# Moving two of seven low-part subtractions per set from VectorE to GpSimd in a fp32 Strassen-Winograd MLP product

## The chip, the cores and the metric

One Trainium2 chip (trn2), one core. The metric is the device time of one execution in microseconds (us), lower is better.

## The reference, cut to what matters

The program is one step of a two-layer backbone on 512 latent and 128 context tokens (640 in all, width 1024). Each layer ends in an MLP with a gated residual:

```python
h2 = _rms_norm(x, lp['norm2_g']) * (1 + sc2) + sh2
x = x + g2 * (jnp.square(jax.nn.relu(h2 @ lp['w_ff1'])) @ lp['w_ff2'])
```

`w_ff1` is 1024 x 4096 and `w_ff2` is 4096 x 1024, all in float32. The change lies in the product with `w_ff2` of the second layer.

## The kernel before, in words

The kernel feeds TensorE with fp32r operands. To keep the precision of a float32 product, it splits each operand in a high part, the value cast to fp32r, and a low part, the value minus its high part. A product is then three matmuls: high by high, high by low, low by high.

**The second MLP.** The second layer's MLP does both of its products in the Strassen-Winograd way: seven block products and a number of block sums take the place of eight block products. The work is 32 *pairs* p (p = 0 to 15 for `w_ff1`, p = 16 to 31 for `w_ff2`), and each pair is seven *products* i = 0 to 6 of 12 matmuls (4 slices of the contraction by 3 parts), so one product is 12 matmuls. A running number w = 7p + i counts the products. The hidden activations of the first product are squared, combined into seven block operands and stored to memory in `hb`. The second product goes through them in four *sets* (c = 0 to 3) of seven *stored blocks* (i = 0 to 6, 128 x 1280 each). Set c is used by the four pairs from p = 16 + 4c on, and its block i is the moving operand of product i of each of them.

**How a set is made ready.** In the pair before the set (p = 15 + 4c) and in the set's first pair, block i is loaded by SP's queue to a stage `FS`, ScalarE casts it to the high part `FB[i][:, 0]` (`block_split`, semaphore `fbh`), and VectorE subtracts to make the low part `FB[i][:, 1]` (`stored_lo`, semaphore `fbv`). TensorE waits for `fbv` before product i of the set's first pair. In what follows, *step r* of a set is the product number counted from the start of pair 15 + 4c: r = 0 to 6 is that pair, and r = 7 + i is the product that first uses block i. The orders are written out by hand: `SPLIT_AT` says at which step ScalarE casts a block, `AT_STEP` at which step VectorE subtracts it (for sets 1 to 3 blocks 0 to 6 at steps 2, 4, 6, 7, 8, 9, 11), and `LATE` by how much the splitting of the weights is held back in these steps.

**What else the engines do.** For each product, VectorE makes the low part of a weight slice (`weight_lo`, `WHL<-RAWB,WHL`, 128 x 512, semaphore `wlo`), for which TensorE waits before each product. These are called WHL r here after the step whose product needs them. In each pair VectorE also forms sums with PSUM: `sums` at i = 3 (`U<-PS,E` and `U<-PS,U`), `lower_right` at i = 5 (`TMP<-PS,U` of L1627, which product 6 of the same pair waits for by `c22`), `upper_right` at i = 6 (`c12`, for product 1 of the next pair) and `lower_left` (`c21`). VectorE runs all of this in one order, as do the others.

**GpSimd.** In pairs p > 16 GpSimd adds three blocks of the pair before into the residual (`residuals(p - 1)`, 128 x 320, L760): the first after ScalarE's first `gated`, the other two after the second. In pairs up to 16 it forms `hidden_sums(p - 1)`, four operations of 128 x 320. For each pair the loop goes on only when these are done. `lower_right(p)` waits by `xup` for the residuals of the pair before.

A stage is used again by a later block. In set 0, where only stages 0 to 3 serve the first seven blocks, the load of block 6 waits for the low part of block 2, in SP's queue between the loads of weights.

Of the kernel before, what the change touches and what calls it, by code (L numbers as in the profile page):

```python
# [7 lines left out]
F32 = mybir.dt.float32  # L8
F32R = mybir.dt.float32r
ALU = mybir.AluOpType  # L10
# [14 lines left out]
H = 4  # L25
# [54 lines left out]
PAIRS7 = 32  # L80
HALF = PAIRS7 // 2
PRODUCTS = 7
SLOTS = 8
BW = 336
SHIFTED = (0, 3, 4, 6)
BX = HT + 2
# [21 lines left out]
def rotations():  # L108
# [27 lines left out]
    ada_mm=8, ada_ev=8, ada_tr=8, mod_done=1, moda_done=2)  # L136

FPER = dict(
    hr=8, hbt=16, hbh=28, hbl=28, sxr=1, sxh=3, sxl=3, whi=7 * PAIRS7, wlo=7 * PAIRS7, pp=7 * PAIRS7,
    e1=PAIRS7, u2=PAIRS7, u4=PAIRS7, c11=PAIRS7, c12=PAIRS7, c21=PAIRS7, c22=PAIRS7, z1=HALF, z2=2 * HALF,  # L140
    fre=PAIRS7, fsq=PAIRS7, ft=4 * HALF, fo0=48 * HALF // 2, fo1=48 * HALF // 2, fs0=80, fs1=80, fs2=80, fs3=64, fs4=48, fs5=48, fs6=48, fbh=28, fbv=28,
    xup=3 * HALF, gt=2 * (HALF - 1), lsq=3)

LENT = dict(
    hr="tap", hbt="taps", hbh="conv", hbl="silu", sxr="csq", sxh="css", sxl="crt", fs3="crr", fs4="o_sq", fs5="o_rt", fs6="ors", whi="kdm", wlo="kde", pp="gce",
# [4 lines left out]
def build(nc, t):  # L150

    ctx = ExitStack()
    with ctx:
# [239 lines left out]
        F = {n: S[x] for n, x in LENT.items()}  # L393
# [27 lines left out]
        def stage(n):  # L421

            return n % 4 if n < PRODUCTS else n % PRODUCTS

        def stage_turn(n):

            return len([x for x in range(n) if stage(x) == stage(n)])
# [66 lines left out]
        with nc.Block() as block:  # L494

            @block.sync
            def _(sp):
# [19 lines left out]
                def fast_loads(l):  # L517

                    b, g0 = fast_base(l), l * CHUNKS + 16

                    def hidden_out(p):

                        c, e = divmod(p, H)
                        done = F["fo1" if p % 2 else "fo0"]
                        sp.wait_ge(F["fsq"], b["fsq"] + 2 * p + 2)
                        sp.dma_start(t["hb"][c, 0, :, e, :], SQ[p % 2][:, 0, 0, :]).then_inc(done, 16)
                        sp.dma_start(t["hb"][c, 1:3, :, e, :].rearrange("b p t -> p b t"), SQ[p % 2][:, 1, :, :]).then_inc(done, 16)
                        sp.wait_ge(F["ft"], b["ft"] + 4 * p + 4)
                        sp.dma_start(t["hb"][c, 3:7, :, e, :].rearrange("b p t -> p b t"), TT4[:, :, :]).then_inc(done, 16)

                    def block_in(n):

                        c, i = divmod(n, PRODUCTS)
                        if i == 0:
                            for x in ("fo0", "fo1"):
                                sp.wait_ge(F[x], b[x] + 48 * (2 * c + 2))
                        if c and i == 4:
                            for x in ("fo0", "fo1"):
                                sp.wait_ge(F[x], b[x] + 24 * HALF)
                        if stage_turn(n):  # L540
                            sp.wait_ge(F["fbv"], b["fbv"] + max(x for x in range(n) if stage(x) == stage(n)) + 1)
                        sp.dma_start(FS[stage(n)][:, :, :], t["hb"][c, STORED[i]]).then_inc(F[f"fs{stage(n)}"], 16)

                    def weights_in(w):

                        p, i = divmod(w, PRODUCTS)
                        if i in PLAIN:
                            src = t["ws"][g0 + p, 32 * PLAIN[i]:32 * PLAIN[i] + 32, :]
                        else:
                            src = t["wp"][SUMMED[i], p]  # L550
                        sp.dma_start(RAWB[:, w % SLOTS, :], src.rearrange("r (a c) -> (r a) c", a=4)).then_inc(slot_in[w % SLOTS], 16)
                    for w in range(SLOTS):
                        if w % 4 == 0:
                            sp.wait_ge(lo_ready, g0 - 1 + w // 4)
                        if w == 1:
                            sp.wait_ge(sums_added, 16 * PAIRS7)
                        weights_in(w)
                    for w in range(7 * PAIRS7):
                        if w + SLOTS < 7 * PAIRS7:
                            sp.wait_ge(F["wlo"], b["wlo"] + w + 1)  # L560
                            weights_in(w + SLOTS)
                        p, i = divmod(w, PRODUCTS)
                        if i == (3 if p == HALF else 5) and 2 <= p < HALF + 2:
                            hidden_out(p - 2)
                        c, k = divmod(w - 7 * (HALF - 3), 28)
                        if 0 <= c < 4:
                            at_step = (6, 8, 10, 12, 22, 23, 23) if c == 0 else (4, 6, 8, 10, 12, 14, 16)
                            for i in range(PRODUCTS):
                                if at_step[i] == k:
                                    block_in(7 * c + i)  # L570
# [149 lines left out]
            def _(pool):  # L720

                def square_sum(n, x, tmp=None, ks=range(KT)):

                    c = squared(n)
                    tmp = TC[0][:, 0:T] if tmp is None else tmp
                    for k in ks:
                        t_ = x(k)
                        if k == 0:
                            nc.gpsimd.tensor_tensor(SQA[:, :], t_, t_, ALU.mult).then_inc(nsq, 1)
                            continue  # L730
                        nc.gpsimd.tensor_tensor(tmp, t_, t_, ALU.mult).then_inc(nsq, 1)
                        pool.wait_ge(nsq, c + 2 * k)
                        nc.gpsimd.tensor_tensor(SQA[:, :], SQA[:, :], tmp, ALU.add).then_inc(nsq, 1)
                        pool.wait_ge(nsq, c + 2 * k + 1)

                def fast_mlp(l, x):
# [25 lines left out]
                    def finished(j, p):  # L762
# [2 lines left out]
                        pool.wait_ge(F["xup"], b["xup"] + 3 * (p - HALF + 1))  # L765
                        square_sum(2 * l + 2, lambda k: flat(X[:, (k % 2) * H + k // 2, :, :]), ks=range(2 * j, 2 * j + 2))
                    square_sum(2 * l + 1, x, SQX[:, :], range(KT - 1))
                    for p in range(PAIRS7):
                        if p > HALF:
                            residuals(p - 1)  # L770
                        if 1 <= p <= HALF:
                            hidden_sums(p - 1)
                        if p > PAIRS7 - 4:
                            finished(p - 1 - (PAIRS7 - 4), p - 1)
# [701 lines left out]
            def _(dve):  # L1476
# [41 lines left out]
                def fast_mlp(l, residual):  # L1518
# [155 lines left out]
                    for w in range(7 * PAIRS7):  # L1674
# [33 lines left out]
                            shift_rest(2, 6, 1).then_inc(F["sxl"], 1)  # L1708
                        c = (p - HALF + 1) // 4
                        rel = w - 7 * (HALF - 1 + 4 * c) if 0 <= c < 4 else -1  # L1710
                        if rel in AT_STEP[c > 0]:
                            stored_lo(7 * c + AT_STEP[c > 0][rel])
                        while low[0] < min(7 * PAIRS7, w + 1 + LO_AHEAD - LATE[c > 0].get(rel, 0)):
                            weight_lo(low[0])
# [554 lines left out]
            def _(pe):  # L2269
# [44 lines left out]
                def fast_mlp(l):  # L2314
# [3 lines left out]
                    def product(w):  # L2318
# [24 lines left out]
                            pe.wait_ge(F["c22"], b["c22"] + p + 1)  # L2343
                        if second and p % 4 == 0:
                            c = (p - HALF) // 4
                            pe.wait_ge(F["fbv"], b["fbv"] + 7 * c + i + 1)
                        out = bank(BANKS[i])[:, 0:n]
                        hi, lo = WHL[:, w % SLOTS, 0, :], WHL[:, w % SLOTS, 1, :]
                        B = HB[i] if first else FB[i]
# [622 lines left out]
```

## Time and profile before

| | us |
|---|---|
| median of 3 runs | 1829.47 (1827.41 to 1832.43) |
| the profiled execution, its own time | 1830.21 |
| its span (first to last instruction) | 1828.4 |
| TensorE busy | 1745.6 (95% of the span) |
| VectorE busy | 1274.1 (70%) |
| ScalarE busy | 841.6 (46%) |
| GpSimd busy | 526.1 (29%) |
| low parts of the stored blocks on VectorE, 28 of them | 1.478 median each |

The span is what the trace covers, and the profiled execution's own time has 1.8 us around it. Busy shares are averages over stages with different limits. The second product of the second MLP runs from 1607.4 to 1813.4 us of the span.

### The profile page before, as it was taken

How to read it: one execution, taken by the hardware profiler on the slowest of the kernel's cores; microseconds unless marked ns; L12 is line 12 of the kernel's file. 1: busy time of each engine (PE TensorE's matmuls, PEld its weight loads, DVE VectorE, ACT ScalarE, POOL GpSimd, SP SyncE). 2: the span in 40 equal slices, each digit the busy share in tenths (PEclk: the TensorE clock that was granted, in tenths of full speed). 3: DMA queues.
4: the chain of work that ended last, by engine and by line, in shares of the span. 5: the costliest groups of instructions: out<-in, count | busy, mean ns of one | idle time of the engine just before them, and what ended most of it. 6: DMA issues, size and time to landing. Idle time of an engine off the chain costs nothing.

```text
span 1828.4 us, 33566 instructions
## 1 busy us (share of the span) xinstructions
PE 1745.6 (95%) x13554; PEld 1659.0 (91%) x13554; DVE 1274.1 (70%) x2127; ACT 841.6 (46%) x1459; POOL 526.1 (29%) x424
## 2 busy tenths in 40 slices
PE   5999999998999999999999999898989999999997
PEld 2989986787999999999999999677889999989997
DVE  2688785688635677676764557666977777788886
ACT  1555327634242231322325653475436666666664
POOL 5000011085442050331551000204832232232225
PEclk9999999989999999999999999998999999999998
DMA  8653223022367869687627761541122677886662
GB/s 345 245 209 95 77 81 59 1 65 88 149 235 209 295 230 321 244 272 273 194 90 203 182 151 47 139 93 42 48 95 90 218 233 256 292 281 245 218 225 88
DMA packets 128038, 316.66 MB, mean 173 GB/s; under 512 B 37829, under 2 KB 64237, under 8 KB 108173
## 3 DMA queue, kind: packets, MB, share of 16 engines
q1 hardware_dynamic: 121740, 279.49, 43.5%
q0 software_dynamic: 4608, 33.56, 9.5%
q8 instruction: 108, 1.77, 0.4%
q10 hardware_dynamic: 1536, 1.48, 0.2%
q14 instruction: 46, 0.37, 0.1%
HBM read 286.01 MB, written 95.49 MB: 209 GB/s over the span
## 4 chain that ended last, share of the span: by engine, by line
PE 78%; DVE 9%; DMA 4%; issue 3%; POOL 3%; ACT 2%; SPq 1%; POOLq 0%; ACTq 0%; DVEq 0%
PE PS L2288 47%; PE PS L2357 17%; DMA ADA<-ada 2%; PE PS L2562 1%; PE PS L2650 1%; POOL FL L911 1%; PE PS L2611 1%; DVE WHL L1544 1%; PE PS L2590 1%; PE PS L2579 1%; PE PS L2724 1%; DVE MPR L1750 1%; PE PS L2425 1%; PE PS L2599 1%; DMA RAWB<-ws 1%
## 5 line engine op out<-in xcount | busy, mean ns | idle before, releaser
L2288 PE MATMUL PS<-HH,HI 128*128 128x320 f32 (+1 forms) x1280 | 300.4, 316 | 4.6 <-DVE HL L1499 4.6
L2288 PE MATMUL PS<-HL,HI 128*128 128x320 f32 (+1 forms) x1280 | 295.9, 313 | 0.0
L2288 PE MATMUL PS<-HH,LO 128*128 128x320 f32 (+1 forms) x1280 | 294.3, 311 | 0.0
L952 ACT CAST HI<-RAW 128x2048 fp32r<-128x2048 f32 x64 | 121.9, 1904 | 273.9 <-PE PS L2288 246.9
L2288 PEld LDWEIGHTS PS<-HH,HI 128*128 128x128 f32 x1280 | 215.8, 191 | 5.2 <-issue 5.1
L2288 PEld LDWEIGHTS PS<-HL,HI 128*128 128x128 f32 x1280 | 219.7, 192 | 0.0
L2288 PEld LDWEIGHTS PS<-HH,LO 128*128 128x128 f32 x1280 | 217.5, 191 | 0.0
L2357 PE MATMUL PS<-FB,WHL 128*128 128x320 f32 x1344 | 199.6, 310 | 6.7 <-DVE TMP L1627 4.3
L2357 PEld LDWEIGHTS PS<-FB,WHL 128*128 128x128 f32 x1344 | 197.1, 188 | 9.1 <-DVE WHL L1544 7.7
L2357 PE MATMUL PS<-HB,WHL 128*128 128x322 f32 (+1 forms) x1344 | 201.5, 313 | 2.4 <-DVE TMP L1627 1.4
L2357 PEld LDWEIGHTS PS<-HB,WHL 128*128 128x128 f32 x1344 | 200.5, 190 | 3.1 <-issue 3.1
L1490 DVE TENSOR_TENSOR LO<-RAW,HI 128x2048 fp32r<-128x2048 f32 (+1 forms) x66 | 155.2, 2352 | 57.5 <-ACT HI L952 57.2
L999 ACT CAST WHL<-RAWB 128x512 fp32r<-128x512 f32 x224 | 137.8, 619 | 112.4 <-PE PS L2357 94.5
L2288 PE MATMUL PS<-FH,HI 128*128 128x320 f32 x768 | 176.6, 311 | 1.6 <-issue 1.6
L1544 DVE TENSOR_TENSOR WHL<-RAWB,WHL 128x512 fp32r<-128x512 f32 x224 | 169.3, 781 | 11.7 <-ACT WHL L999 10.0
L2288 PE MATMUL PS<-FH,LO 128*128 128x320 f32 x768 | 175.1, 309 | 0.0
L2288 PE MATMUL PS<-FL,HI 128*128 128x320 f32 x640 | 146.4, 310 | 0.0
L1750 DVE SCALAR_TENSOR_TENSOR MPR<-WM,CB 128x1024 f32<-128x1024 f32 x96 | 137.9, 1436 | 11.2 <-DMA WM<-adt 9.5
L2288 PEld LDWEIGHTS PS<-FH,HI 128*128 128x128 f32 x768 | 128.5, 189 | 2.0 <-issue 1.1
L2288 PEld LDWEIGHTS PS<-FH,LO 128*128 128x128 f32 x768 | 128.7, 188 | 0.0
L2288 PEld LDWEIGHTS PS<-FL,HI 128*128 128x128 f32 x640 | 107.5, 189 | 0.0
L928 POOL TENSOR_TENSOR TC<-TC 128x640 f32<-128x640 f32 x32 | 50.4, 1576 | 181.1 <-ACT FH L1435 181.1
(347 smaller groups left out, 2902.7 us busy)
## 6 DMA issues: line engine op xcount, KB each, us to landing
RAW<-ws SPq DMA_DIRECT2D x64, 1024.0 KB, 5.1
wp<-ws SPq DMA_DIRECT2D x32, 1024.0 KB, 8.2
RAWB<-wp SPq DMA_DIRECT2D x128, 256.0 KB, 3.9
WM<-adt SPq DMA_DIRECT2D x48, 512.0 KB, 9.4
RAWB<-ws SPq DMA_DIRECT2D x96, 256.0 KB, 3.6
FS<-hb SPq DMA_DIRECT2D x28, 640.0 KB, 8.0
ADA<-ada SPq DMA_DIRECT2D x16, 1024.0 KB, 7.7
wp<-ws POOLq DMA_DIRECT2D x16, 1024.0 KB, 10.1
```

What stands on the lines that cost most here:

```text
L911: last = nc.gpsimd.tensor_tensor(grp(halves(FL, j), g), nat(ATT[:, j, :], g, g * LAT), grp(halves(FH, j), g).bitcast(F32), ALU.subtract)
L928: nc.gpsimd.tensor_tensor(TC[u][:, 0:T], TC[u][:, 0:T], TC[u][:, 0:T], ALU.mult).then_inc(S["f1_sq"], 1)
L952: nc.scalar.copy(HI[g % 2][:, :], RAW[g % 2][:, :]).then_inc(hi_ready, 1)
L999: nc.scalar.copy(WHL[:, w % SLOTS, 0, :], operand(w)).then_inc(F["whi"], 1)
L1490: last = nc.vector.tensor_tensor(LO[g % 2][:, c], RAW[g % 2][:, c], HI[g % 2][:, c].bitcast(F32), ALU.subtract)
L1544: nc.vector.tensor_tensor(WHL[:, w % SLOTS, 1, :], operand(w), WHL[:, w % SLOTS, 0, :].bitcast(F32), ALU.subtract).then_inc(F["wlo"], 1)
L1750: return nc.vector.scalar_tensor_tensor(out=MPR[:, :], in0=w[:, :], scalar=1.0, in1=cond[:, g, :], op0=ALU.mult, op1=ALU.mult, accum_out=M ...
L2288: last = pe.matmul(bank(2 * u + a)[:, 0:e], w[:, cols], m[:, a * HT:a * HT + e], start=(k == 0 and f), stop=(k == KT - 1 and e_))
L2357: last = pe.matmul(out, x[:, cols], B[:, y, k, 0:n], start=(opens and k == 0 and v == 0), stop=(k == H - 1 and v == 2), skip_group_check=n ...
L2425: last = pe.matmul(bank(7)[:, 464 + i * NB + b:465 + i * NB + b], SQT[i % 2][:, c.start - 1:c.stop - 1], one, start=True, stop=True)
L2562: pe.matmul(pair(0)[:, 0:LAT], q, kt[:, 0:LAT], start=True, stop=True)
L2579: last = pe.matmul(bank(7 if i else 2)[:, c:c + hi - lo], TSQ[rows, p, toks(b)], KSW[rows, lo:hi], start=True, stop=True)
```

## The change

Of the seven stored blocks of a set, blocks 2 and 5 (`POOLED`) get their low part on GpSimd: eight subtractions of 128 x 1280 in all. VectorE's order leaves these two steps out and is otherwise the same. In GpSimd's loop, at the set's first pair (p = 16, 20, 24, 28), block 2 stands ahead of that iteration's residual additions, and block 5 behind them and ahead of the hidden sums (of p = 16 alone, where there are no additions yet). The new subtractions count on the semaphore `hbt`. TensorE and SP wait for whichever semaphore the block now has (`low_done`).

```diff
+POOLED = (2, 5)
...
+        def low_done(b, n):
+
+            c, i = divmod(n, PRODUCTS)
+            if i in POOLED:
+                return F["hbt"], b["hbt"] + 16 + len(POOLED) * c + POOLED.index(i) + 1
+            return F["fbv"], b["fbv"] + (PRODUCTS - len(POOLED)) * c + i + 1 - len([x for x in POOLED if x < i])
...
-                            sp.wait_ge(F["fbv"], b["fbv"] + max(x for x in range(n) if stage(x) == stage(n)) + 1)
+                            sp.wait_ge(*low_done(b, max(x for x in range(n) if stage(x) == stage(n))))
...
+                    def stored_lo(n):
+
+                        i = n % PRODUCTS
+                        pool.wait_ge(F["fbh"], b["fbh"] + n + 1)
+                        nc.gpsimd.tensor_tensor(FB[i][:, 1, :, :], FS[stage(n)][:, :, :], FB[i][:, 0, :, :].bitcast(F32),
+                                                ALU.subtract).then_inc(F["hbt"], 1)
                     for p in range(PAIRS7):
+                        c, first = divmod(p - HALF, H)
+                        if c >= 0 and first == 0:
+                            stored_lo(PRODUCTS * c + POOLED[0])
                         if p > HALF:
                             residuals(p - 1)
+                        if c >= 0 and first == 0:
+                            stored_lo(PRODUCTS * c + POOLED[1])
                         if 1 <= p <= HALF:
                             hidden_sums(p - 1)
...
-                        if rel in AT_STEP[c > 0]:
+                        if rel in AT_STEP[c > 0] and AT_STEP[c > 0][rel] not in POOLED:
                             stored_lo(7 * c + AT_STEP[c > 0][rel])
...
-                            pe.wait_ge(F["fbv"], b["fbv"] + 7 * c + i + 1)
+                            pe.wait_ge(*low_done(b, 7 * c + i))
```

## Rows read from the trace of the kernel before

**Rows 1.** The chain of work that ended last: share of the span by engine

```profile
PE 78%; DVE 9%; DMA 4%; issue 3%; POOL 3%; ACT 2%; SPq 1%; POOLq 0%; ACTq 0%; DVEq 0%
```

**Rows 2.** Busy time by stretch: length, then PE, PEld, DVE, ACT, POOL, clock, DMA

```profile
1675.00:1697.00 22.00, 22.00 (x152) 22.00 (x151) 16.24 (x29) 11.22 (x22) 5.69 (x6) 1.00 0.97 359
1697.00:1725.00 28.00, 26.99 (x183) 26.52 (x182) 24.26 (x35) 20.60 (x32) 7.93 (x6) 1.00 0.43 141
```

**Rows 3.** Timeline of TensorE, second product: start, us, what [idle before]

```profile
1607.43 8.96 PE L2357 MATMUL PS<-FB,WHL 128*128 128x320 f32 x60
1617.05 2.03 PE L2357 MATMUL PS<-FB,WHL 128*128 128x320 f32 x12 [0.66 <-DVE WHL L1544]
1620.22 24.86 PE L2357 MATMUL PS<-FB,WHL 128*128 128x320 f32 x168 [1.15 <-DVE FB L1667]
...
1710.21 12.55 PE L2357 MATMUL PS<-FB,WHL 128*128 128x320 f32 x84 [0.80 <-DVE TMP L1627]
1722.98 37.18 PE L2357 MATMUL PS<-FB,WHL 128*128 128x320 f32 x252 [0.22 <-issue]
```

**Rows 4.** The low parts of the stored blocks, all 28: min/median/max ns

```profile
L1667 DVE TENSOR_TENSOR FB<-FS,FB x28: 1471/1478/2164, 1597.5 to 1770.4; 128x1280 fp32r<-128x1280 f32 x28
```

**Rows 5.** Timeline of VectorE around set 2

```profile
1707.59 1.48 DVE L1667 TENSOR_TENSOR FB<-FS,FB 128x1280 fp32r<-128x1280 f32 x1
1708.99 0.68 DVE L1544 TENSOR_TENSOR WHL<-RAWB,WHL 128x512 fp32r<-128x512 f32 x1
1709.59 0.47 DVE L1627 TENSOR_TENSOR TMP<-PS,U 128x320 f32<-128x320 f32 x1
...
1710.58 0.67 DVE L1544 TENSOR_TENSOR WHL<-RAWB,WHL 128x512 fp32r<-128x512 f32 x1
...
1713.38 4.28 DVE L1667 TENSOR_TENSOR FB<-FS,FB 128x1280 fp32r<-128x1280 f32 x3
...
1718.61 1.18 DVE L1544 TENSOR_TENSOR WHL<-RAWB,WHL 128x512 fp32r<-128x512 f32 x1
1719.71 2.16 DVE L1667 TENSOR_TENSOR FB<-FS,FB 128x1280 fp32r<-128x1280 f32 x1
...
1722.40 0.47 DVE L1627 TENSOR_TENSOR TMP<-PS,U 128x320 f32<-128x320 f32 x1
```

**Rows 6.** Timeline of ScalarE around set 2

```profile
1706.94 1.27 ACT L1071 CAST FB<-FS 128x1280 fp32r<-128x1280 f32 x1
...
1716.35 1.01 ACT L1079 ACTIVATE TMP<-TMP,MOD 128x512 f32<-128x512 f32 x2
```

**Rows 7.** Timeline of GpSimd around set 2: first and third residual addition

```profile
1715.67 2.73 POOL L760 TENSOR_TENSOR X<-X,TMP 128x320 f32<-128x320 f32 x1 [8.56 <-ACT TMP L1079]
...
1719.20 1.32 POOL L760 TENSOR_TENSOR X<-X,TMP 128x320 f32<-128x320 f32 x1
```

**Rows 8.** GpSimd's subtractions in the first MLP, its residual additions: min/median/max ns

```profile
L931 POOL TENSOR_TENSOR FL<-TC,FH x32: 1559/1578/2432, 525.3 to 908.8; 128x640 fp32r<-128x640 f32 x32
...
L760 POOL TENSOR_TENSOR X<-X,TMP x45: 870/882/2728, 1625.7 to 1806.1; 128x320 f32<-128x320 f32 x45
```

**Rows 9.** Timelines of VectorE and GpSimd behind set 0

```profile
1625.41 1.97 DVE L1544 TENSOR_TENSOR WHL<-RAWB,WHL 128x512 fp32r<-128x512 f32 x2
...
1625.68 1.15 POOL L760 TENSOR_TENSOR X<-X,TMP 128x320 f32<-128x320 f32 x1 [1.35 <-ACT TMP L1079]
```

**Rows 10.** Timelines of GpSimd, ScalarE and VectorE at set 0

```profile
1605.82 1.40 POOL L752 TENSOR_TENSOR TT<-SQ,TT 128x320 f32<-128x320 f32 x1
...
1613.42 1.25 ACT L1071 CAST FB<-FS 128x1280 fp32r<-128x1280 f32 x1
...
1614.90 1.49 DVE L1667 TENSOR_TENSOR FB<-FS,FB 128x1280 fp32r<-128x1280 f32 x1
1616.31 1.28 DVE L1544 TENSOR_TENSOR WHL<-RAWB,WHL 128x512 fp32r<-128x512 f32 x2
```

**Rows 11.** DMA issues from 1608 to 1611 us: count, KB each, us to landing

```profile
FS<-hb SPq DMA_DIRECT2D x1, 640.0 KB, 5.2
```

More of the change, by code:

```diff
@@ L138 @@
 FPER = dict(
-    hr=8, hbt=16, hbh=28, hbl=28, sxr=1, sxh=3, sxl=3, whi=7 * PAIRS7, wlo=7 * PAIRS7, pp=7 * PAIRS7,
+    hr=8, hbt=16 + 4 * len(POOLED), hbh=28, hbl=28, sxr=1, sxh=3, sxl=3, whi=7 * PAIRS7, wlo=7 * PAIRS7, pp=7 * PAIRS7,
     e1=PAIRS7, u2=PAIRS7, u4=PAIRS7, c11=PAIRS7, c12=PAIRS7, c21=PAIRS7, c22=PAIRS7, z1=HALF, z2=2 * HALF,
-    fre=PAIRS7, fsq=PAIRS7, ft=4 * HALF, fo0=48 * HALF // 2, fo1=48 * HALF // 2, fs0=80, fs1=80, fs2=80, fs3=64, fs4=48, fs5=48, fs6=48, fbh=28, fbv=28,
+    fre=PAIRS7, fsq=PAIRS7, ft=4 * HALF, fo0=48 * HALF // 2, fo1=48 * HALF // 2, fs0=80, fs1=80, fs2=80, fs3=64, fs4=48, fs5=48, fs6=48, fbh=28, fbv=28 - 4 * len(POOLED),
     xup=3 * HALF, gt=2 * (HALF - 1), lsq=3)
```

## The prediction

> **What bounds the kernel now.** I read the chain that ended last first: TensorE holds 78% of it [rows 1]. A cut on another engine pays only where TensorE waits for it. The stretches show where that is [rows 2]: between two sets TensorE is busy for 22.00 of 22.00 us, and in the stretch around set 2 for 26.99 of 28.00 us, with the clock at 1.00 in both. So the timeline of TensorE comes next [rows 3]. From step 6 of set 2 it runs 84 matmuls in 12.55 us, or 1.79 us for a product of 12, and around the sets it waits. In set 0 it waits 0.66 us at step 12 (the 60 matmuls of steps 7 to 11 end at 1616.4) and 1.15 us at step 13. In set 2 it waits 0.80 us ahead of step 6 and 0.22 us ahead of step 13, and sets 1 and 3 repeat set 2 with other offsets. The 0.80 us end with VectorE's L1627 of step 5, which stands behind block 1 and a weight [rows 5]; both stay on VectorE. What the change could give back is thus 0.66 + 1.15 + 3 x 0.22 = 2.5 us at most. This is under 0.3% of the time (5.5 us), about what a measurement of this kernel can tell from no change.
>
> **What is removed.** Eight subtractions of 1.48 us [rows 4] leave VectorE: 11.8 us of its time. By itself this is worth at most the 2.5 us above, for elsewhere TensorE is behind its own work.
>
> **What is added, and its length.** GpSimd gets eight subtractions of 128 x 1280, which it hasn't done before. Its nearest row is the same operation with the same types on 128 x 640: 1.56 us undisturbed. A two-input operation on 128 x 320 takes 0.87 us [rows 8]. So 320 elements cost 0.69 us, and 1280 make 1.56 + 2 x 0.69 = 2.94 us. The bounds are 1.56 (no longer than half the elements) and 3.12 us (twice the half); 1.56 would mean that the growth from 320 to 640 stops there, so I take 2.94.
>
> **The two engines shut each other out.** In set 2 GpSimd's first addition began at 1715.67 and took 2.73 us where 0.88 is usual [rows 7, 8]; VectorE's three subtractions in a row meanwhile ran unstretched until 1717.66 [rows 5]. Then it was VectorE's turn to lose: the weight at 1718.61 took 1.18 us for 0.67, and block 6 at 1719.71 took 2.16 for 1.48 [rows 4, 5], while GpSimd's additions ran. The excess of each is the other's remainder, to about 0.1 us. VectorE's operations with PSUM show no such stretch (0.47 us). I take from this that an operation of GpSimd and one of VectorE with both inputs in SBUF don't run side by side, and that the one that comes second waits for the whole of the first.
>
> The Trainium skill says so too (SBUF — State Buffer, SBUF: two separate sides): the port pair that VectorE and GpSimd share is an exclusive lock, and a VectorE instruction with two SBUF inputs is among those that want it. By that rule moving work from VectorE to GpSimd frees VectorE of 1.48 us and blocks it for GpSimd's whole operation; the trace agrees, with the 2.73 us above. Without the lock the sum would be the 3 us of the second rival, with it the 7.3 us below.
>
> **Block 2 in sets 1 to 3.** In set 2 its cast ends at 1706.94 + 1.27 = 1708.21 [rows 6], and GpSimd has done the additions of the pair before. But VectorE subtracts block 1 until 1709.07, and the weight WHL 10 follows at once until 1709.67 [rows 5]. Which of the two gets the turn at 1709.0 is open. In favour of VectorE: at 1716.2 GpSimd had waited for 0.5 us, and VectorE's next block still went first (2.73 us) [rows 7]. In favour of GpSimd: at 1626.1 it had waited for 0.4 us and got in between two weights, which took 1.97 us instead of 1.3 [rows 9]. Block 1 is of the first kind, long and with the next instruction ready, so I let VectorE go first. Then GpSimd runs from about 1709.6 to 1712.5. L1627 reads PSUM and isn't held up. Behind it the next weight at 1710.58 waits until 1712.4 and ends at 1713.05; upper_right ends at 1713.5, in time for step 8 at 1713.8. Block 2 is due at 1715.6. Cost: nothing, hidden behind steps 6 to 8 with 0.2 us to spare. If GpSimd goes first, WHL 10 and L1627 end 2.7 us later, and TensorE's step 6 with them: 2.7 us a set.
>
> **Block 5 in sets 1 to 3.** It stands behind three additions. The first begins when block 4 on VectorE ends (now about 1716.6, as blocks 3 and 4 run 0.4 us later than before without block 2) and ends at 1717.4. The other two want ScalarE's second product with the gate, done at 1716.35 + 1.01 = 1717.36 [rows 6], and take until 1717.4 + 2 x 0.87 = 1719.1. The weight WHL 12, ready at 1718.61, waits for that and runs to 1719.6. Then block 5 takes until 1719.5 + 2.94 = 1722.45. Step 12 was at 1710.21 + 6 x 1.79 = 1720.95; with 0.15 us of signal, as from L1627's end at 1710.06 to 1710.21, it starts at 1722.6, or 1.65 us late. Behind block 5 VectorE has block 6 (until 1723.8), WHL 13 (1724.4) and L1627 (1724.8), in one queue; TensorE's step 13 waits for the last, so it starts at 1724.95 instead of 1722.98: 2.0 us late a set, the stall at step 12 included. If block 6 goes ahead of block 5, both come later by 1.5 to 2 us, 3.9 us a set; if the lock costs nothing, 1.0 us (second rival). Later steps follow with the same shift, as TensorE ran 252 matmuls without a wait behind it [rows 3], so nothing gives this back.
>
> **Set 0.** There are no additions, so block 2 starts when GpSimd's hidden sums end at 1607.2 and ends at 1610.2, before step 9 at 1611.0; VectorE's block 3 waits behind it, but is due only at 1612.8. SP's load of block 6 now waits for this end instead of VectorE's at 1608.7; it takes 5.2 us [rows 11] and lands at 1615.4, before its cast at 1617.3, so I cost it at nothing (it would cost TensorE directly if it landed 2 us later). Block 5's cast ends at 1613.42 + 1.25 = 1614.67 [rows 10]; GpSimd subtracts until 1617.6. VectorE, without block 5 at 1614.90, wants the weight of step 12 at once, but is shut out until 1617.6 and ends it at 1618.2. Step 12 starts at 1618.35 instead of 1617.05: 1.3 us, and step 13 follows between 0.85 and 1.7 us late. I take 1.3.
>
> **The sum.** 3 x 2.0 + 1.3 = 7.3 us. The profiled execution took 1830.21 us (its span 1828.4), so it would take 1837.5; it stands 0.74 us above the median of the runs. From the median I predict 1829.5 + 7.3 = 1836.8 us.
>
> **Rivals.**
>
> *GpSimd goes first with block 2.* Its 2.7 us ahead of step 6 come on top of block 5's wait, which stays at 2.0 us: 4.7 x 3 + 1.3 = 15.4 us, 1844.9 us. For it speaks the case at 1626 us, against it the one at 1716 us. All three sets should go the same way, as their offsets are alike.
>
> *The lock costs nothing at the critical places.* Then block 5 still can't start before the additions end at 1719.1, and ends at 1722.0; step 12 comes 1.2 us and step 13 1.0 us late, and in set 0 step 12's 0.7 us vanish in the old wait at step 13. The sum is 3 x 1.0 = 3.0 us, 1832.5 us, within 0.3%. Against it stand the stretched rows; for it, that VectorE's operations with PSUM fill part of these steps and aren't stretched.
>
> *GpSimd is in time, not slower.* If its subtraction takes under 1.8 us (from 1719.1 to 1720.9), block 5 is there at step 12, the earlier VectorE wins the 2.5 us, and the time is 1827.0 us. The 1.56 us for half the elements speaks against it.
>
> *The change does nothing for TensorE either way* would need both waits hidden; the additions ahead of block 5 exclude it unless the operation is as short as in the last rival.
>
> **Chances and range.** The forecast 0.47, GpSimd first 0.30, no lock 0.18, in time 0.05. The forecast itself lies between 4.5 us (0.8 less for each set) and 13 us (block 6 goes first: 3 x 3.9 + 1.3), so a sixth of it, 0.08, falls within 0.3%. Faster by over 0.3% would need 5.5 us where 2.5 are to be had: 0.02. Within 0.3%: 0.18 + 0.05 + 0.08 - 0.02 = 0.29. Slower: the rest, 0.69. The range of 8 in 10 runs from just below the no-lock case, 1832.0, to above GpSimd first with 0.7 us more a set, 1847.0; of the likeliest alone it is 1834 to 1842.
>
> **What would show it.** In the changed profile: GpSimd's 128 x 1280 subtractions of about 2.9 us, longer where VectorE had the turn; VectorE's weights stretched to 2 us and more behind them; TensorE waiting 1.6 us at step 12 of sets 1 to 3 and L1627 behind block 6 ahead of step 13; no longer wait ahead of step 6 (a wait of 3.5 us there is the first rival); in set 0 a wait of about 2 us at step 12 for a weight. The prediction is wrong if GpSimd's operation is much shorter or longer than 2.94 us (0.1 us of it is 0.4 us of the sum), if the additions end earlier than 1719.1, or if VectorE's queue falls behind by so much that weights come late in later pairs, which the DMA's long stretches could turn into further waits.

## The result and the profile after

The changed kernel takes 1853.89 us (median of 4 runs, 1852.97 to 1855.22) beside 1830.11 us of the kernel before in the same session (4 runs): a ratio of 1.0129 [1.0114, 1.0144], slower by 23.8 us. The forecast was 1836.8 us in a range of 1832.0 to 1847.0: the direction was right, and the time lies 6.9 us outside the range. The profiled execution took 1853.50 us with a span of 1851.7 us, so its span is 23.3 us longer than before.

The lines of the kernel have moved: L1686 is VectorE's low part of a block (L1667 before), L780 GpSimd's, L1563 the low part of a weight, L1646 `lower_right`, L768 the residual additions and L2376 TensorE. In the other runs they shift again, by a few lines.

Timeline of TensorE in the changed kernel, second product, from step 12 of set 0 to behind set 2 (answers to [rows 3]):

```profile
1618.03 2.02 PE L2376 MATMUL PS<-FB,WHL 128*128 128x320 f32 x12 [1.89 <-DVE WHL L1563]
1621.26 37.32 PE L2376 MATMUL PS<-FB,WHL 128*128 128x320 f32 x252 [1.20 <-DVE FB L1686]
1662.08 13.47 PE L2376 MATMUL PS<-FB,WHL 128*128 128x320 f32 x72 [3.50 <-DVE TMP L1646]
1677.17 2.00 PE L2376 MATMUL PS<-FB,WHL 128*128 128x320 f32 x12 [1.62 <-POOL FB L780]
1679.48 37.18 PE L2376 MATMUL PS<-FB,WHL 128*128 128x320 f32 x252 [0.31 <-issue]
1720.16 13.45 PE L2376 MATMUL PS<-FB,WHL 128*128 128x320 f32 x72 [3.50 <-DVE TMP L1646]
1735.23 2.00 PE L2376 MATMUL PS<-FB,WHL 128*128 128x320 f32 x12 [1.62 <-POOL FB L780]
1737.54 37.18 PE L2376 MATMUL PS<-FB,WHL 128*128 128x320 f32 x252 [0.31 <-issue]
1778.22 13.43 PE L2376 MATMUL PS<-FB,WHL 128*128 128x320 f32 x72 [3.51 <-DVE TMP L1646]
```

Three things are to be seen. Ahead of step 6 of each later set TensorE now waits 3.50 us. Behind that wait the 72 matmuls of steps 6 to 11 take 13.45 us, though the same number took 72/84 of 12.55 = 10.76 us before [rows 3]. And step 12 waits 1.62 us, this time for GpSimd. For set 1, whose rows of before don't stand above, the timeline of TensorE in the kernel before had this:

```profile
1645.68 12.55 PE L2357 MATMUL PS<-FB,WHL 128*128 128x320 f32 x84 [0.59 <-DVE TMP L1627]
1659.48 12.55 PE L2357 MATMUL PS<-FB,WHL 128*128 128x320 f32 x84 [1.25 <-DVE TMP L1627]
```

Timeline of VectorE in the changed kernel around set 2: block 1, the weight of step 10, `lower_right` of step 5; further on the weight of step 12 and block 6 (answers to [rows 5]):

```profile
1714.83 1.48 DVE L1686 TENSOR_TENSOR FB<-FS,FB 128x1280 fp32r<-128x1280 f32 x1
1716.23 3.38 DVE L1563 TENSOR_TENSOR WHL<-RAWB,WHL 128x512 fp32r<-128x512 f32 x1
1719.54 0.48 DVE L1646 TENSOR_TENSOR TMP<-PS,U 128x320 f32<-128x320 f32 x1
...
1731.18 1.12 DVE L1563 TENSOR_TENSOR WHL<-RAWB,WHL 128x512 fp32r<-128x512 f32 x1
1732.23 4.21 DVE L1686 TENSOR_TENSOR FB<-FS,FB 128x1280 fp32r<-128x1280 f32 x1
```

Timeline of GpSimd in the same stretch: block 2, the last two additions, block 5 (answers to [rows 7]):

```profile
1715.52 3.55 POOL L780 TENSOR_TENSOR FB<-FS,FB 128x1280 fp32r<-128x1280 f32 x1 [1.16 <-ACT FB L1090]
...
1730.04 1.71 POOL L768 TENSOR_TENSOR X<-X,TMP 128x320 f32<-128x320 f32 x2 [0.88 <-ACT TMP L1098]
1731.72 3.36 POOL L780 TENSOR_TENSOR FB<-FS,FB 128x1280 fp32r<-128x1280 f32 x1
```

Block 2 is there at 1715.52, while VectorE still subtracts block 1. When block 1 ends at 1716.31, GpSimd goes first, and the weight of step 10, which stands next on VectorE (1716.23), needs 3.38 us instead of 0.68. `lower_right` stands behind it, and TensorE's step 6 waits for `lower_right`.

Busy time by stretch in the changed kernel, behind the wait of set 2: length, then PE, PEld, DVE, ACT, POOL, granted clock, DMA (answers to [rows 2]):

```profile
1720.00:1722.00 2.00, 1.84 (x7) 1.87 (x8) 1.60 (x5) 0.00 (x0) 0.00 (x0) 0.50 0.37 131
1722.00:1725.00 3.00, 3.00 (x13) 3.00 (x12) 1.26 (x2) 1.21 (x2) 0.00 (x0) 0.50 0.40 93
1725.00:1728.00 3.00, 3.00 (x19) 3.00 (x18) 2.04 (x2) 1.96 (x5) 0.00 (x0) 0.82 0.01 3
1728.00:1731.00 3.00, 3.00 (x23) 3.00 (x22) 0.83 (x2) 2.56 (x6) 1.84 (x3) 1.00 0.00 0
```

After the wait TensorE has the granted clock 0.50, the lower of its two levels (1.2 GHz), and 1.00 (2.4 GHz) again later; 0.82 is a mean of the two. At 0.50 it does 13 matmuls in 3 us, at 1.00 it does 23.

**Where the 23.3 us are.** From step 6 of set 0 to the end of the last product it took 1813.58 - 1605.56 = 208.0 us before and takes 1835.56 - 1605.32 = 230.2 us now: 22.2 us more. They are, set by set from the rows above:

| place | us |
|---|---|
| wait ahead of step 6: 3.50 + 3.50 + 3.51 instead of 1.25 + 0.80 + 0.79 | +7.7 |
| steps 6 to 11 at half clock: 13.47 + 13.45 + 13.43 instead of 3 x 10.76 | +8.1 |
| step 12: 3 x 1.62 of wait, and 2.00 for the 12 matmuls that start anew instead of 1.79 | +5.5 |
| step 13: 3 x 0.31 instead of 0.21 + 0.22 + 0.21 | +0.3 |
| set 0: 1.89 and 1.20 instead of 0.66 and 1.15 | +1.3 |
| the wait of 0.59 us between sets 0 and 1 that is gone, and 0.1 more in the last pair | -0.5 |

This makes 22.4, within 0.2 us of the 22.2. The rest of the span, 1.3 us behind the last product less 0.2 us ahead of set 0, lies where the change does nothing. Behind the last product TensorE is busy for 6.70 us instead of 5.40, at a mean clock of 0.60 instead of 0.68: its last two groups of ten small matmuls take 2.04 and 2.39 us instead of 1.26 and 1.86, which is these 1.3 us. The 2.39 us also stand in `writes_without_reads` below, which is as fast as the kernel before, so that part, 0.5 us, can't be put down to the change.

### The profile page after: what moved, and what is told of

Same layout as the page of the kernel before. It is cut to its first block, busy times and chain, and to the rows that moved or that the text cites. A ratio compares the mean times of both kernels' runs of the same rounds, so it can differ in the third digit from the quotient of the medians.

```text
span 1851.7 us, 33566 instructions
## 1 busy us (share of the span) xinstructions
PE 1751.8 (95%) x13554; PEld 1665.9 (90%) x13554; DVE 1282.3 (69%) x2119; ACT 842.0 (45%) x1459; POOL 545.9 (29%) x432
## 3 DMA queue, kind: packets, MB, share of 16 engines
q10 hardware_dynamic: 1536, 1.48, 0.2%
## 4 chain that ended last, share of the span: by engine, by line
PE 77%; DVE 9%; issue 4%; POOL 3%; DMA 3%; ACT 2%; SPq 1%; POOLq 0%; DVEq 0%; ACTq 0%
PE PS L2307 46%; PE PS L2376 18%; DMA ADA<-ada 2%; PE PS L2581 1%; DVE WHL L1563 1%; POOL FL L930 1%; PE PS L2630 1%; PE PS L2609 1%; PE PS L2669 1%; PE PS L2598 1%; PE PS L2743 1%; DVE MPR L1769 1%; PE PS L2444 1%; PE PS L2618 1%; PE PS L2642 1%
## 5 line engine op out<-in xcount | busy, mean ns | idle before, releaser
L2376 PE MATMUL PS<-FB,WHL 128*128 128x320 f32 x1344 | 208.2, 317 | 20.4 <-DVE TMP L1646 11.5
L2376 PEld LDWEIGHTS PS<-FB,WHL 128*128 128x128 f32 x1344 | 205.1, 195 | 23.3 <-DVE WHL L1563 16.2
L2376 PE MATMUL PS<-HB,WHL 128*128 128x322 f32 (+1 forms) x1344 | 201.3, 312 | 2.6 <-DVE TMP L1646 1.4
L2376 PEld LDWEIGHTS PS<-HB,WHL 128*128 128x128 f32 x1344 | 200.3, 190 | 3.3 <-issue 3.3
L1563 DVE TENSOR_TENSOR WHL<-RAWB,WHL 128x512 fp32r<-128x512 f32 x224 | 179.4, 826 | 9.6 <-ACT WHL L1018 8.1
L1769 DVE SCALAR_TENSOR_TENSOR MPR<-WM,CB 128x1024 f32<-128x1024 f32 x96 | 137.9, 1437 | 11.8 <-DMA WM<-adt 10.1
```

What stands on the lines that cost most here:

```text
L1563: nc.vector.tensor_tensor(WHL[:, w % SLOTS, 1, :], operand(w), WHL[:, w % SLOTS, 0, :].bitcast(F32), ALU.subtract).then_inc(F["wlo"], 1)
L1769: return nc.vector.scalar_tensor_tensor(out=MPR[:, :], in0=w[:, :], scalar=1.0, in1=cond[:, g, :], op0=ALU.mult, op1=ALU.mult, accum_out=M ...
L2376: last = pe.matmul(out, x[:, cols], B[:, y, k, 0:n], start=(opens and k == 0 and v == 0), stop=(k == H - 1 and v == 2), skip_group_check=n ...
```

## The experiments

Ratios are against the kernel before, run beside each. "Held" below means the time that one engine shuts the other out.

### The two blocks apart

`block5_alone` leaves block 2 on VectorE, `block2_alone` block 5; the rest is as in the changed kernel.

```diff
-POOLED = (2, 5)
+POOLED = (5,)      # block5_alone: behind the additions; block2_alone has (2,), ahead of them
...
```

> Only block 5 goes to GpSimd, block 2 stays on VectorE. Theory (GpSimd takes its turn between block 1 and the next weight on VectorE, TensorE pauses for 3.5 us ahead of step 6, and its clock falls for that pause): no extra pause ahead of step 6 (0.8 us as before), the clock stays at 1.00 between the sets, block 5 costs 1.6 to 2.0 us in each of sets 1 to 3 and 1.2 us in set 0, in all 6 to 8 us: 1836 to 1838 us. Rival (the clock falls for the pause of 1.6 us at step 12, or for anything else that came with the change): the half clock shows in this run too and the time is 1843 us or more.

> Only block 2 goes to GpSimd. Theory: the pause of 3.5 us ahead of step 6 in sets 1 to 3 stays, with the fall of the clock behind it (2.7 + 2.7 us a set, 16 us), no wait at step 12 for GpSimd, set 0 as before or 0.5 us better: 1845 to 1847 us. Rival (block 2 and block 5 hurt only together, or the fall of the clock belongs to block 5): 1838 us or less.

With block 5 alone the time is 1837.56 us, ratio 1.0037 [1.0023, 1.0052]; with block 2 alone 1843.02 us, ratio 1.0067 [1.0043, 1.0091]. TensorE's timelines, first block 5 alone, then block 2 alone:

```profile
1713.42 10.80 PE L2374 MATMUL PS<-FB,WHL 128*128 128x320 f32 x72 [0.79 <-DVE TMP L1644]
1725.84 2.00 PE L2374 MATMUL PS<-FB,WHL 128*128 128x320 f32 x12 [1.62 <-POOL FB L780]
1728.15 37.18 PE L2374 MATMUL PS<-FB,WHL 128*128 128x320 f32 x252 [0.31 <-issue]
```

```profile
1663.61 52.14 PE L2374 MATMUL PS<-FB,WHL 128*128 128x320 f32 x336 [3.50 <-DVE TMP L1644]
1719.25 51.03 PE L2374 MATMUL PS<-FB,WHL 128*128 128x320 f32 x336 [3.50 <-DVE TMP L1644]
1773.78 26.41 PE L2374 MATMUL PS<-FB,WHL 128*128 128x320 f32 x168 [3.50 <-DVE TMP L1644]
```

The waits belong to the blocks one by one: 3.50 us to block 2, 1.62 us to block 5. The half clock goes with the 3.50 us (72 matmuls take 10.80 us behind a wait of 0.79). Here it took less than in the changed kernel: 336 matmuls at full clock are 4 x 12.55 = 50.2 us, so 1.9, 0.8 and 1.3 us went; why the clock came back sooner here, no run tells. The execution in this trace took 1846.05 us, within the 1845 to 1847 us expected, but it was the slowest of four: the median is 2 us under what I expected, and there is no trace of a faster one.

### Is it the wait that halves the clock?

`filled_pause` is the changed kernel with 20 matmuls of no use in TensorE ahead of step 6, so that the wait is as long, but TensorE works in it.

```diff
 if i == 6:
+    if p in (19, 23, 27):
+        for _ in range(20):
+            pe.matmul(bank(7)[:, 0:HT], WHL[:, w % SLOTS, 0, 0:P], WHL[:, w % SLOTS, 0, 0:HT], start=True, stop=True)
     pe.wait_ge(F["c22"], b["c22"] + p + 1)
```

> The changed kernel, and TensorE runs 20 matmuls of no use (operands that are there, a bank of PSUM that nobody reads) in its pause ahead of step 6 of sets 1 to 3. Nothing else is altered, step 6 can start no earlier. Theory (the idle pause lets the clock fall, which costs 2.7 us a set behind it): granted clock 1.00 in steps 6 to 11, their 72 matmuls take 10.8 us instead of 13.5, and the time falls by 8 us to 1845.8 us. Rival (the fall has another cause): 1853 to 1854 us and the half clock as before.

It takes 1846.37 us, ratio 1.0086 [1.0065, 1.0108], so 7.5 us less than the changed kernel with 60 matmuls more. TensorE's timeline, and the busy time of the stretch behind it:

```profile
1656.79 3.10 PE L2364 MATMUL PS<-WHL 128*128 128x320 f32 x20
1660.44 10.82 PE L2380 MATMUL PS<-FB,WHL 128*128 128x320 f32 x72 [0.55 <-DVE TMP L1646]
```

```profile
1660.40:1671.30 10.90, 10.82 (x72) 10.55 (x72) 8.31 (x11) 7.22 (x12) 4.50 (x4) 1.00 0.20 51
```

The wait for VectorE is about the same (1660.44 - 1656.79 = 3.65 us), but the clock stays at 1.00 and the 72 matmuls take 10.82 us, in all three sets (10.82, 10.82 and 10.83). So the 8.1 us are the price of an idle TensorE, and they come on top of the wait itself.

### Does GpSimd hold VectorE for one instruction?

`halves` cuts each of GpSimd's subtractions into two of 128 x 640.

```diff
...
-nc.gpsimd.tensor_tensor(FB[i][:, 1, :, :], FS[stage(n)][:, :, :], FB[i][:, 0, :, :].bitcast(F32), ALU.subtract).then_inc(F["hbt"], 1)
+for h in (slice(0, 2), slice(2, 4)):
+    nc.gpsimd.tensor_tensor(FB[i][:, 1, h, :], FS[stage(n)][:, h, :], FB[i][:, 0, h, :].bitcast(F32), ALU.subtract).then_inc(F["hbt"], 1)
```

> The changed kernel with each of GpSimd's subtractions cut in two of 128 x 640 (1.56 us each by the rows of the first MLP). Theory (the turn at the SBUF port is held for one instruction): VectorE gets the weight of step 10 in behind the first half, so the pause ahead of step 6 is about 0.8 + 1.35 = 2.2 us instead of 3.5; block 6 on VectorE gets in between the halves of block 5, so the wait at step 12 grows to about 3 us and the one at step 13 goes. Whether the clock falls for pauses of 2.2 and 3 us is open; without it 1843 to 1846 us, with it up to 1853. Rival (the turn is held until GpSimd has nothing waiting): pauses as before, 1853 us.

It takes 1851.96 us, ratio 1.0119 [1.0106, 1.0133]. TensorE's timeline in set 1:

```profile
1662.54 10.79 PE L2377 MATMUL PS<-FB,WHL 128*128 128x320 f32 x72 [2.16 <-DVE TMP L1647]
1676.34 41.56 PE L2377 MATMUL PS<-FB,WHL 128*128 128x320 f32 x264 [3.01 <-POOL FB L781]
```

The wait ahead of step 6 shrinks to 2.16 us, as the weight of step 10 now waits for one half (2.03 us instead of 3.38) and gets its turn between the two. But block 5 pays: VectorE gets in between its halves too, and step 12 waits 3.01 us. The lock is held for one instruction, and what is cut up loses its place. The total hardly falls, since TensorE's clock now drops behind the three waits of 3.01 us and behind one of the three of 2.15 us: the 264 matmuls above take 41.56 us where 22 products of 1.79 us would be 39.4.

`port_held_without_use` and `writes_without_reads` are the kernel before with an operation of no use on GpSimd in sets 1 and 2, at the place of block 2, for which no other engine waits. The first reads constants and subtracts, the second only writes.

```diff
 ...
+if p in (20, 24):
+    pool.wait_ge(F["fbh"], b["fbh"] + 7 * (p - HALF) // 4 + 3)
+    nc.gpsimd.tensor_tensor(DUM[:, :], K[:, 0:1152], K[:, 0:1152], ALU.subtract) ...   # port_held_without_use
+    for k in range(3): nc.gpsimd.memset(DUM[:, :], 0.0) ...                            # writes_without_reads
     ...
```

> The kernel before, with all low parts on VectorE, and in sets 1 and 2 GpSimd subtracts 128 x 1152 constants into a place that nobody reads, at the point where the change has block 2 (2.65 us long by the same slope). No other engine waits for it. Theory (it is the turn at the port that hurts, not data that come late): TensorE pauses 0.8 + 2.4 = 3.2 us ahead of step 6 in sets 1 and 2, set 3 as before; with half clock behind the pauses between 0.8 and 2.7 us each, 1836 to 1840 us. Rival (block 2 on GpSimd hurts since its result comes late): 1830 us, as before.

> The same, but GpSimd runs three memsets of 128 x 1152 into the unused place instead, about 1 us each, one after the other: it writes SBUF and reads none. Theory in the form of the Trainium skill (VectorE with two SBUF inputs is shut out only by a GpSimd operation that reads SBUF): the pause ahead of step 6 stays 0.8 us and the time 1830 us. Rival (any work of GpSimd in SBUF shuts VectorE out): WHL 10 is stretched by up to 1 us and step 6 late by as much in sets 1 and 2, 1832 us or more, and the stretch shows in the rows.

The first takes 1836.05 us, ratio 1.0033 [1.0023, 1.0043]; the second 1831.28 us, ratio 1.0001 [0.9992, 1.001]. Timelines of all engines in set 2 give GpSimd's operation and VectorE's block 1 and weight, first with the subtraction, then with the writes:

```profile
1710.32 1.48 DVE L1672 TENSOR_TENSOR FB<-FS,FB 128x1280 fp32r<-128x1280 f32 x1
...
1711.02 2.74 POOL L772 TENSOR_TENSOR DUM<-K 128x1152 f32<-128x1152 f32 x1 [1.18 <-ACT FB L1076]
...
1711.72 2.59 DVE L1549 TENSOR_TENSOR WHL<-RAWB,WHL 128x512 fp32r<-128x512 f32 x1
```

```profile
1706.84 1.48 DVE L1673 TENSOR_TENSOR FB<-FS,FB 128x1280 fp32r<-128x1280 f32 x1
...
1707.52 3.30 POOL L773 MEMSET DUM<- 128x1152 f32 x3 [1.16 <-ACT FB L1077]
...
1708.24 0.68 DVE L1550 TENSOR_TENSOR WHL<-RAWB,WHL 128x512 fp32r<-128x512 f32 x1
```

The subtraction that nobody needs makes the weight 2.59 us and step 6 wait 2.71 us in both sets (0.80 in set 3, where it isn't done); three writes of 3.30 us together make no difference. The 2.71 us are less than the 3.2 expected because this subtraction of constants ran only 1.96 us past block 1's end (1711.02 + 2.74 - 1711.80), where block 2 ran 2.76 us past it in the changed kernel. So it is no dependence on block 2 that delays step 6, but the reading GpSimd. The Trainium skill (SBUF — State Buffer, SBUF: two separate sides) says that a VectorE operation with two SBUF inputs contends only with a GpSimd operation that reads SBUF; these two runs agree with it.

### Who gets the turn

`block2_a_little_later` and `block2_much_later` are the changed kernel with a clearing of 128 x 256 and of 128 x 704 unused elements in front of block 2's subtraction in sets 1 to 3. `three_arrivals` and `arrivals_late` are the kernel before with a subtraction of no use at block 2's place behind nothing or a clearing; each set has a size of its own.

```diff
 if c >= 0 and first == 0:
+    if c:
+        pool.wait_ge(F["fbh"], b["fbh"] + PRODUCTS * c + POOLED[0] + 1)
+        nc.gpsimd.memset(DUM[:, 0:256], 0.0)        # much later: 0:704
     stored_lo(PRODUCTS * c + POOLED[0])
```

> As the changed kernel, but in sets 1 to 3 GpSimd clears 128 x 256 unused elements (an operation without an SBUF input, about 0.3 us) between block 2's cast and its subtraction, and nothing else waits for that. My reading of the rows: who gets the turn is settled before VectorE's running instruction ends; GpSimd got in when it came at most 0.70 us after that instruction had begun, and not when it came 0.79 us after or later. Block 2 came 0.69 us after block 1 had begun; 0.3 us later it should lose the turn to the weight of step 10: the pause ahead of step 6 is 0.8 us in place of 3.5, the clock doesn't fall, and the kernel with a longer GpSimd path is some 16 us faster: about 1837.5 us. Rival: GpSimd gets the turn at any end of a VectorE instruction for which it waits at all; then the pause is 3.5 us again, the clock falls, and the time is about 1854 us.

> The kernel before, with a subtraction of 128 x 896 constants on GpSimd at block 2's place in sets 1, 2 and 3 that nobody waits for: in set 1 at once after block 2's cast, in set 2 behind a clearing of 128 x 32 elements (estimate 0.1 to 0.2 us), in set 3 behind one of 128 x 256 (0.3 us). If the turn is settled some 0.7 us after block 1 begins, set 1 has a weight of step 10 of about 2 us and a pause of 2.1 us ahead of step 6, set 3 has 0.68 and 0.80 us, and set 2 is on the edge. Rival (any wait is enough): all three sets have the long weight and the pause.

> As the run with block 2 a little later, but with 128 x 704 elements cleared (estimate 0.7 us): GpSimd then comes about 1.3 us after block 1 has begun, some 0.1 to 0.2 us before its end. If there is a point near the end from which VectorE's next instruction goes first, the weight of step 10 takes 0.68 us, the pause ahead of step 6 is 0.8 us, and the time about 1838 us. If any wait is enough for GpSimd: weight about 3.1 us, pause 3.5 us (what GpSimd loses by the clearing is hidden in block 1), about 1853 us.

> The kernel before, with a short subtraction of 128 x 288 constants (about 0.8 us) that nobody waits for, behind clearings of 128 x 384, 576 and 768 elements in sets 1, 2 and 3: it comes about 1.1, 1.25 and 1.4 us after block 1 has begun. If there is a point before the end, one or more of the sets show a weight of step 10 of 0.68 us and a pause of 0.80 us, the later ones first. If any wait is enough, all three weights take 1.2 to 1.5 us and the pauses are 1.3 to 1.6 us.

The two with the real subtraction take 1853.17 us, ratio 1.0127 [1.011, 1.0144], and 1853.01 us, ratio 1.0114 [1.0097, 1.0131]; the others, one execution each, 1834.66 and 1827.46 us. My reading fell. GpSimd coming 0.94 us after block 1's beginning got the turn (weight 3.38 us, wait 3.50 us in all three sets), in `three_arrivals` all three sets waited 2.28 us, and in the run with the clearing of 704 elements it still got it at 1714.45 - 1713.12 = 1.33 us, as GpSimd's block 2 and VectorE's weight in set 2 show (`block2_much_later`, timelines of both engines):

```profile
1714.45 2.91 POOL L781 TENSOR_TENSOR FB<-FS,FB 128x1280 fp32r<-128x1280 f32 x1
...
1714.53 3.38 DVE L1567 TENSOR_TENSOR WHL<-RAWB,WHL 128x512 fp32r<-128x512 f32 x1
```

The edge shows in `arrivals_late`. Timelines of all engines, GpSimd's short subtraction and VectorE's block 1 and weight, in set 2 and in set 3:

```profile
1703.65 1.48 DVE L1673 TENSOR_TENSOR FB<-FS,FB 128x1280 fp32r<-128x1280 f32 x1
...
1704.87 0.79 POOL L773 TENSOR_TENSOR DUM<-K 128x288 f32<-128x288 f32 x1
...
1705.05 1.15 DVE L1550 TENSOR_TENSOR WHL<-RAWB,WHL 128x512 fp32r<-128x512 f32 x1
...
1754.85 1.48 DVE L1673 TENSOR_TENSOR FB<-FS,FB 128x1280 fp32r<-128x1280 f32 x1
...
1756.23 1.23 POOL L773 TENSOR_TENSOR DUM<-K 128x288 f32<-128x288 f32 x1
...
1756.25 0.68 DVE L1550 TENSOR_TENSOR WHL<-RAWB,WHL 128x512 fp32r<-128x512 f32 x1
```

At 1.22 us after block 1's beginning GpSimd goes first and the weight takes 1.15 us; at 1.38 us, 0.10 us before block 1 ends, the weight goes first (0.68 us) and GpSimd waits (1.23 us for 0.79). So behind block 1 GpSimd went first when it was there 0.15 us or more before VectorE's instruction ended, and not at 0.10 us, as if the weight weren't in line until then. Between two blocks it was otherwise in two places: VectorE kept the turn at 1716.2 of the kernel before [rows 5, 7], where GpSimd had come 0.9 us after block 4's beginning, and in `block5_alone_first` below, at 0.8 us after block 3's. In `block2_alone_after_step5` GpSimd came 0.43 us after block 4's beginning (1714.61 - 1714.18) and did get in ahead of block 5. Why a second block holds the turn from some point on and a weight hardly does, no run here tells.

### Other places for the two blocks

`block2_after_step5` holds block 2 back until `lower_right` of step 5 is done; `block2_alone_after_step5` does that and leaves block 5 on VectorE. `block5_alone_first` has block 5 alone, but ahead of the additions; `both_well_placed` holds block 2 back and puts block 5 right behind it.

```diff
 if c >= 0 and first == 0:
+    pool.wait_ge(F["c22"], b["c22"] + p)            # block 2 held back
     stored_lo(PRODUCTS * c + POOLED[0])
+    stored_lo(PRODUCTS * c + POOLED[1])             # both_well_placed: block 5 ahead of the additions
 if p > HALF:
     residuals(p - 1)
 ...
```

> Both blocks on GpSimd, but block 2 starts only when VectorE's lower_right of step 5 is done, so that it can't get in between block 1 and that. Theory: step 6 waits 0.8 us as before, the clock stays at 1.00, what is left is block 5: 6 to 8 us, 1836 to 1838 us, about what the prediction forecast. Rival (the delay ahead of step 6 doesn't come from the turn at the shared SBUF port but from a load or a cast that is late): TensorE still pauses, 1845 us or more.

> Only block 2 on GpSimd, and it starts after lower_right of step 5. Theory: GpSimd's operation is hidden behind steps 6 to 8, VectorE's freed 1.48 us are worth nothing to TensorE but some tenths at step 13, set 0 within 1 us of before: 1829 to 1831 us, no change that can be measured. Rival (the freed time of VectorE is worth something once GpSimd is out of the way): 1827.5 us or less.

> Block 5 alone on GpSimd, ahead of the three residual additions. My theory: what made step 12 of sets 1 to 3 wait 1.62 us is that block 5 stood behind additions that end at about 1.7 us past their second gate. Its cast ends about 5 us before step 12 is due, so ahead of the additions it is done in time: no wait at step 12 of sets 1 to 3 (under 0.3 us), set 0 as with block 5 alone (1.2 us more), 1830 to 1833 us. Rival: the wait is the price of the subtraction itself, which shuts VectorE out of block 6 and the weights wherever it stands, so a like wait only moves to another step: 1.5 us a set, about 1836 to 1838 us as with block 5 behind the additions.

> Both blocks on GpSimd, block 2 held back until VectorE's lower_right of step 5 is done, block 5 right behind it and ahead of the additions. My theory: neither the 3.5 us ahead of step 6 nor the 1.62 us at step 12 are left; what stays is set 0 (1.3 us) and about 1 us a set that block 2 was seen to cost even when it is held back: 1832 to 1835 us, not faster than the kernel before. Rival one (VectorE's freed 3 us a set are worth something once the places are right): 1828 us or less. Rival two (two operations of 2.9 us close together shut VectorE out so long that weights come late): 1837 us or more.

| run | us | ratio |
|---|---|---|
| `block2_after_step5` | 1837.50 | 1.0045 [1.0029, 1.006] |
| `block2_alone_after_step5` | 1835.29 | 1.0026 [1.0015, 1.0037] |
| `block5_alone_first` | 1836.67 | 1.0031 [1.0019, 1.0043] |
| `both_well_placed` | 1838.39 | 1.0037 [1.0025, 1.005] |

With block 2 held back the 3.50 us are gone and TensorE's timeline in set 2 is what the prediction described, to 1.71 us at step 12; the time is near the 1836.8 us forecast:

```profile
1713.93 3.75 PE L2377 MATMUL PS<-FB,WHL 128*128 128x320 f32 x24 [0.80 <-DVE TMP L1647]
1717.88 7.27 PE L2377 MATMUL PS<-FB,WHL 128*128 128x320 f32 x48 [0.19 <-issue]
1726.87 2.00 PE L2377 MATMUL PS<-FB,WHL 128*128 128x320 f32 x12 [1.71 <-POOL FB L780]
```

One thing I had expected didn't hold: in set 0 the clock fell to 0.50 behind the wait of 1.89 us at step 12, and step 13 and what follows took 39.35 us instead of 37.18. `both_well_placed` shows the same (39.28 us). TensorE's timeline in set 0 of `block2_after_step5`:

```profile
1620.58 39.35 PE L2377 MATMUL PS<-FB,WHL 128*128 128x320 f32 x252 [0.96 <-DVE FB L1687]
```

The other three miss the times I expected, and in each a wait moves; two of them came out where their rival said (`block5_alone_first` at 1836 to 1838 us, `both_well_placed` at 1837 or more), the third above both of its cases. Block 2 held back and alone was to cost nothing, and costs 1.0 us a set in its trace. VectorE's timeline in set 2 shows the weight of step 11 and the two last of the chain that step 13 waits for:

```profile
1708.96 3.09 DVE L1562 TENSOR_TENSOR WHL<-RAWB,WHL 128x512 fp32r<-128x512 f32 x1
...
1721.20 0.68 DVE L1562 TENSOR_TENSOR WHL<-RAWB,WHL 128x512 fp32r<-128x512 f32 x1
1721.80 0.47 DVE L1645 TENSOR_TENSOR TMP<-PS,U 128x320 f32<-128x320 f32 x1
```

VectorE is held for 3.09 - 0.68 = 2.4 us and freed of 1.48, so it is about 1 us behind at the next `lower_right`: that ends 13.67 us after TensorE's step 6 (1722.27 - 1708.60), where it ended 12.66 us after it before (1722.87 - 1710.21) [rows 3, 5].

Block 5 ahead of the additions is ready for step 12, but now the additions are late. Timelines of GpSimd and VectorE in set 1: block 5 waits 2 us for VectorE's blocks 3 and 4, the additions end at 1674.2, and `lower_right` waits for them:

```profile
1664.64 4.92 POOL L780 TENSOR_TENSOR FB<-FS,FB 128x1280 fp32r<-128x1280 f32 x1 [7.05 <-ACT FB L1088]
1669.50 4.70 POOL L768 TENSOR_TENSOR X<-X,TMP 128x320 f32<-128x320 f32 x3
```

```profile
1663.85 2.88 DVE L1684 TENSOR_TENSOR FB<-FS,FB 128x1280 fp32r<-128x1280 f32 x2
...
1674.30 0.49 DVE L1644 TENSOR_TENSOR TMP<-PS,U 128x320 f32<-128x320 f32 x1 [0.82 <-POOL X L768]
```

TensorE then waits 1.66 us at step 13 instead of 1.62 at step 12. With both well placed, VectorE's blocks 3 and 4 take 6.16 us for 2.88, and TensorE waits 0.69 us at step 11 and 0.42 at step 13. No order that I tried makes the change worth its price.

## Why the prediction was wrong

**What bounds, and what there was to gain: right as far as the runs go.** Freeing VectorE of up to 11.8 us made no run faster than the kernel before. One reading was loose: set 1 doesn't repeat set 2, its step 6 waited 1.25 us before and not 0.80, so a wait of 3.50 us adds 2.25 us there.

**The length of GpSimd's subtraction: right.** Forecast 2.94 us. The eight in the changed kernel take 2.93 at least, and 2.96 to 2.98 where GpSimd didn't have to wait, in sets 1 to 3 of `both_well_placed`.

**The exclusive turn: right,** and confirmed from a new side by the subtraction of no use and by the writes.

**"Block 1 is of the first kind, long and with the next instruction ready, so I let VectorE go first": the step that failed.** GpSimd went first in all three sets. The wait ahead of step 6 grew from 0.8 to 3.50 us, the 2.7 us that the first rival priced, with the sign in the profile that the prediction named for it. I had one case for each order and took a likeness in length as the reason; the runs show that VectorE's weight behind a block doesn't hold the turn until 0.1 us before the block ends. Held back from this place (`block2_after_step5`), the same change takes 1837.50 us, near the forecast.

**A term that was missing altogether.** Neither the forecast nor the rival had a price for what the wait itself does to TensorE: 2.7 us a set at half clock, 8.1 us in all. The first rival gave 1844.9 us, inside the range; with the wait filled by work the kernel takes 1846.37, and without it 1853.89. The prediction read a granted clock of 1.00 in the stretches around the sets [rows 2] and did not ask what a wait four times as long would make of it, though the profile of the kernel before has a mean clock of 0.8 in two of its forty slices, ahead of this product.

**Block 5 in sets 1 to 3: right in size.** 1.62 us at step 12 (forecast 1.65) and 1.93 us a set in all (5.8 / 3; forecast 2.0), though from other terms: step 13 waits only 0.1 us longer than before, not 0.35, and 0.2 us go because TensorE starts step 12 anew, so that the sums agree is in part luck. Its cause, the additions ahead of it, was only half of it: without them in front the same 1.6 us come at the next step.

**Set 0: right,** 1.28 us (forecast 1.3), with step 12 at 1.89 us for the weight. That it agrees to 0.02 us is luck: the wait at step 13 alone is 1.15 us in the kernel before and 1.64 us in `writes_without_reads`, where set 0 is the same.

**A slip in the sum for the range.** 0.8 us less for each set makes 3 x 1.2 + 1.3 = 4.9 us and not 4.5; next to nothing hangs on it.

## What to carry to other kernels

Moving a two-input operation from VectorE to GpSimd did not free VectorE here: it was held for GpSimd's longer operation (2.4 us for 1.48 us given up), and what stood next in its queue paid. When you price a new wait of an engine that sets the time, price the time behind the wait too: here a wait of 3.5 us cost another 2.7 us a set at half clock (0.8 to 1.9 us in `block2_alone`). And where the order of two engines at a shared resource decides and the rows show both orders, a likeness to one of them is no reason: give the undecided case its full price, or hold the operation back so that the order can't matter.

## What the hardware showed that I had not expected

In the second product TensorE's clock fell in or just behind every wait of 3.0 us and more, 15 of 15 in the runs above, and stayed at 0.50 for some 3.4 to 6.8 us. With shorter waits it went either way: it fell in one of the two of 2.71 us, in two of the three of 2.28 us, in one of the three of 2.15 and 2.16 us, in two of the eight from 1.88 to 2.03 us in set 0, and in none of those of 1.6 to 1.8 us. The Trainium skill (TensorE: Matmul & The Clock Gate, Part 1: The HAM clock gate) says that the low level is the default and activity lifts it; the stretches at 0.50 behind a wait and 1.00 after some us of work agree.

That GpSimd takes the turn from a weight that VectorE has next in its own order, even when it comes only 0.15 us before the running block ends, and yet not always from a second block that follows the first, I had not expected either; what decides between two blocks stays open.
